# Four K pairs of each up strip by seven products instead of three, two remainders by an adding transfer

## The reference, cut to what matters

```python
# x: (1, 256, 2048) float32
h = h + 0.5 * rms_norm(swiglu(rms_norm(h, ffn1_pre), ffn1_up, ffn1_down), ffn1_post)
mix = hybrid_mixer(rms_norm(h, mix_pre), w_in, ...)      # pooling, window attention, retention; gated merge
h = h + rms_norm(mix, mix_post)
h = h + 0.5 * rms_norm(swiglu(rms_norm(h, ffn2_pre), ffn2_up, ffn2_down), ffn2_post)

def swiglu(x, w_up, w_down):                             # w_up: 2048 x 11264, w_down: 5632 x 2048
    g, u = jnp.split(x @ w_up, 2, axis=-1)
    return (jax.nn.silu(g) * u) @ w_down
```

## Time and profile before

| | us |
|---|---|
| median of 3 runs | 2365.75 (2365.57 to 2366.02) |
| the profiled execution | 2365.93 |
| its span, first to last instruction | 2364.2 |
| up loop of the first FFN, about | 60 to 477 |
| up loop of the second FFN, about | 1710 to 2127 |

### The profile page before, as it was taken

The page is one execution under the profiler, slowest core; times in us unless marked ns, Lnnn a source line. Parts: engine busy times, 40 slices in busy tenths (PEclk is TensorE's granted clock), DMA queues, the critical chain, the costliest instruction groups (busy, mean ns, idle before and its releaser), DMA issues. The chain is left out here.

```text
span 2364.2 us, 34093 instructions
## 1 busy us (share of the span) xinstructions
PE 2349.9 (99%) x10579; PEld 1938.5 (82%) x10579; DVE 1823.2 (77%) x2163; ACT 1265.4 (54%) x1519; POOL 207.0 (9%) x402
## 2 busy tenths in 40 slices
PE   9999999999999999999999999999999999999998
PEld 7888888888888888888888888888888888888887
DVE  5999999978876655656675767665799999997886
ACT  6555555555545554454555544544655555555553
POOL 1212112110000000000000000000021212111000
PEclk9999999999999999999999999999999999999999
DMA  7666676665676565565565566666666666666665
GB/s 236 218 212 206 216 222 215 220 214 192 207 242 210 159 182 172 160 188 158 178 200 192 195 195 203 194 240 198 204 210 225 213 214 207 218 213 214 205 204 196
DMA packets 267183, 481.64 MB, mean 204 GB/s; under 512 B 21217, under 2 KB 54673, under 8 KB 265457
## 3 DMA queue, kind: packets, MB, share of 16 engines
q1 hardware_dynamic: 252752, 453.04, 59.5%
q0 software_dynamic: 14192, 27.73, 3.5%
q10 hardware_dynamic: 176, 0.07, 0.0%
HBM read 462.93 MB, written 6.29 MB: 198 GB/s over the span
## 5 line engine op out<-in xcount | busy, mean ns | idle before, releaser
L1382 ACT ACTIVATE w_hi<-w_raw 128x1024 fp32r<-128x1024 f32 (+1 forms) x848 | 857.4, 1015 | 926.1 <-PE acc L843 627.9
L1778 DVE TENSOR_TENSOR w_lo<-w_raw,w_hi 128x1024 fp32r<-128x1024 f32 (+1 forms) x848 | 984.2, 1164 | 420.0 <-ACT w_hi L1382 415.5
L841 PE MATMUL acc<-w_hi,xT_hi 128*128 128x512 f32 x1376 | 540.9, 393 | 1.2 <-DVE w_lo L1778 1.0
L843 PE MATMUL acc<-w_hi,xT_lo 128*128 128x512 f32 x1376 | 535.9, 389 | 0.0
L842 PE MATMUL acc<-w_lo,xT_hi 128*128 128x512 f32 x1376 | 535.7, 389 | 0.0
L841 PEld LDWEIGHTS acc<-w_hi,xT_hi 128*128 128x128 f32 x1376 | 258.3, 188 | 56.7 <-issue 3.0
L843 PEld LDWEIGHTS acc<-w_hi,xT_lo 128*128 128x128 f32 x1376 | 258.3, 188 | 54.4
L842 PEld LDWEIGHTS acc<-w_lo,xT_hi 128*128 128x128 f32 x1376 | 258.4, 188 | 52.2
L753 POOL DMA_DIRECT2D act_raw<-blocks x352 | 174.9, 497 | 736.3 <-DVE blocks L2114 646.9
L841 PE MATMUL acc<-w_hi,act_hi 128*128 128x512 f32 x560 | 218.2, 390 | 0.1
L842 PE MATMUL acc<-w_lo,act_hi 128*128 128x512 f32 x560 | 217.9, 389 | 0.0
(11 more groups left out here) (321 smaller groups left out, 2866.0 us busy)
## 6 DMA issues: line engine op xcount, KB each, us to landing
w_raw<-in_ffn_up_dram SPq DMA_DIRECT2D x352, 512.0 KB, 4.2
w_raw<-in_ffn_down_dram SPq DMA_DIRECT2D x176, 512.0 KB, 4.2
w_raw<-in_w_gate_dram SPq DMA_DIRECT2D x96, 512.0 KB, 4.4
w_raw<-in_w_in_dram SPq DMA_DIRECT2D x72, 512.0 KB, 3.7
w_raw<-in_w_in_dram SPq DMA_DIRECT2D x128, 256.0 KB, 3.0
w_raw<-in_w_ret_out_dram SPq DMA_DIRECT2D x32, 512.0 KB, 4.1
w_raw<-in_w_out_dram SPq DMA_DIRECT2D x32, 512.0 KB, 4.5
act_raw<-blocks POOLq DMA_DIRECT2D x352, 32.0 KB, 3.8
```

Source lines behind the costliest of these rows:

```text
L841: pe.matmul(pair[m][:, :], xh, wh, start=(first and kk == 0), stop=False)
L843: mm = pe.matmul(pair[m][:, :], xl, wh, start=False, stop=(last and kk == KG - 1))
L1382: act.activation(w_hi[:, s, cols], w_raw[:, s, cols], ACT.Copy).then_inc(w_rounded, 1)
L1778: dve.tensor_tensor(w_lo[:, s, cols], w_raw[:, s, cols], w_hi[:, s, cols].bitcast(f32), ALU.subtract).then_inc(w_split, 1)
```

## The change

QUADS gets a fourth entry, and the strip a new order: gate groups 0 to 3 plain, upper group 4 plain, quads (5, 6) and (7, 8), upper group 9 plain, quads (10, 11) and (12, 13), upper groups 14 and 15 plain. The remainders of groups 9 and 14 are no longer made by DVE: their raw weights go by SP into buffers of their own (`far_raw`), ACT writes the rounded weights and also their negative (`far_lo` = -hi), and POOL issues a transfer from `far_raw` to `far_lo` that adds (raw - hi). These are issued behind `turn_hidden` of the strip. PE waits for them ahead of groups 9 and 14 (`far_added`). The two sets of t buffers alternate, and `s_hi` and `far_lo` lie where `h` is at other times.

```diff
-QUADS = ((5, 6, 5), (9, 10, 6), (12, 13, 7))
-PLAIN_GATE = ((0, 0), (1, 1), (2, 2), (3, 3), (4, 4))
-PLAIN_UP = ((7, 0), (8, 1), (11, 2), (14, 3), (15, 4))
+QUADS = ((5, 6, 4), (7, 8, 5), (10, 11, 6), (12, 13, 7))
+ADDED = {9: (6, 1), 14: (10, 7)}
+PLAIN_GATE = ((0, 0), (1, 1), (2, 2), (3, 3))
+PLAIN_UP = ((4, 0), (9, 1), (14, 2), (15, 3))
...
-        T_SLOT = (1, 0, 1)
+        T_SLOT = (0, 1, 0, 1)
...
+                        if n in ADDED_LOAD:
+                            j = ADDED_AT[ADDED_LOAD[n]]
+                            sp.wait_ge(w_used, group(f"up{f}", i, ADDED_LOAD[n]) - 2 * GD + 1 + SLOTS)
+                            sp.dma_start(far_raw[j][:, :].rearrange("p (kk n) -> p kk n", kk=KG),
+                                         cols(ADDED_LOAD[n])).then_inc(far_landed[j], 16)
+                        if n in ADDED:
+                            sp.wait_ge(w_split, group(f"up{f}", i, n) + 1)
+                            sp.sem_inc(w_landed[n % SLOTS], 16)
+                        else:
+                            load(f"up{f}", i, n, cols(n))
...
+            def add_raw(f, i, n):
+
+                j = ADDED_AT[n]
+                pool.wait_ge(far_negated[j], strip_no(f"up{f}", i) + 1)
+                pool.sem_inc(far_begun, 1)
+                pool.dma_start(far_lo[j][:, :].bitcast(f32), far_raw[j][:, :], accum_op=ALU.add).then_inc(far_added[j], 16)
...
-            with pool.Fori(0, NUP) as p:
-                turn_hidden(0, p)
+            with pool.Fori(0, NST) as i:
+                turn_hidden(0, i)
+                for n in ADDED:
+                    add_raw(0, i, n)
+            turn_hidden(0, NST)
...
                         if n in up_of:
                             s, k = n % SLOTS, KG * up_of[n]
+                            if k == 0:
+                                pe.wait_ge(acc_read[pair_of(sec, 1)], strip_in_pair(sec, i, 1) + 1)
                             pe.wait_ge(w_split, group(sec, i, n) + 1 + SLOTS)
+                            if added(sec, n):
+                                pe.wait_ge(w_rounded, group(sec, i, n) + 1)
+                                pe.wait_ge(far_added[ADDED_AT[n]], 16 * (strip_no(sec, i) + 1))
...
+                    if added(sec, ahead):
+                        j = ADDED_AT[ahead]
+                        act.wait_ge(far_landed[j], 16 * (strip_no(sec, i) + 1))
+                        act.wait_ge(w_used, group(sec, i, ahead) + 1)
+                        act.activation(w_hi[:, s, :], far_raw[j][:, :], ACT.Copy).then_inc(w_rounded, 1)
+                        return
...
                         round_group(sec, i, n)
+                        if n in ADDED_NEGATE:
+                            j = ADDED_AT[ADDED_NEGATE[n]]
+                            act.wait_ge(far_landed[j], 16 * (strip_no(sec, i) + 1))
+                            act.wait_ge(w_used, group(sec, i, ADDED_NEGATE[n]) - 2 * GD + 1 + SLOTS)
+                            act.activation(far_lo[j][:, :], far_raw[j][:, :], ACT.Copy, scale=-1.0).then_inc(far_negated[j], 1)
...
                 s, cols = n % SLOTS, w_cols(sec, i, n + SLOTS)
+                if added(sec, n + SLOTS):
+                    return
+                groups = 2 if added(sec, n + SLOTS + 1) else 1
                 dve.wait_ge(w_rounded, group(sec, i, n + SLOTS) + 1)
-                dve.tensor_tensor(w_lo[:, s, cols], w_raw[:, s, cols], w_hi[:, s, cols].bitcast(f32), ALU.subtract).then_inc(w_split, 1)
+                dve.tensor_tensor(w_lo[:, s, cols], w_raw[:, s, cols], w_hi[:, s, cols].bitcast(f32),
+                                  ALU.subtract).then_inc(w_split, groups)
```

More of the change, by code:

```diff
@@ L51 @@
 WARM_UP = 2
-QUADS = ((5, 6, 5), (9, 10, 6), (12, 13, 7))
-PLAIN_GATE = ((0, 0), (1, 1), (2, 2), (3, 3), (4, 4))
-PLAIN_UP = ((7, 0), (8, 1), (11, 2), (14, 3), (15, 4))
+QUADS = ((5, 6, 4), (7, 8, 5), (10, 11, 6), (12, 13, 7))
+ADDED = {9: (6, 1), 14: (10, 7)}
+ADDED_LOAD = {at: n for n, (at, neg) in ADDED.items()}
+ADDED_NEGATE = {at: n for n, (load, at) in ADDED.items()}
+ADDED_AT = {n: j for j, n in enumerate(ADDED)}
+PLAIN_GATE = ((0, 0), (1, 1), (2, 2), (3, 3))
+PLAIN_UP = ((4, 0), (9, 1), (14, 2), (15, 3))
 NQUAD = len(QUADS)
@@ L254, in hybrid_trunk @@
         s_lo = sb("s_lo", [P, 4, NQUAD, P], f32r, at=s_x)
-        s_hi = sb("s_hi", [P, 4, NQUAD, P], f32r, at=s_x + 16 * NQUAD * P)
-        assert s_x + 32 * NQUAD * P <= r_end
+        s_hi = sb("s_hi", [P, 4, NQUAD, P], f32r, at=x_at - 4 * MT * D)
+        assert s_x + 16 * NQUAD * P <= r_end
+        far_raw = [sb("far_raw0", [P, KG * STRIP], f32, at=s_x + 16 * NQUAD * P),
+                   sb("far_raw1", [P, KG * STRIP], f32, at=r_hi - 4 * KG * STRIP)]
+        far_at = x_at - 4 * MT * D + 16 * NQUAD * P
+        far_lo = [sb(f"far_lo{j}", [P, KG * STRIP], f32r, at=far_at + 4 * KG * STRIP * j) for j in range(len(ADDED))]
+        assert s_x + 16 * NQUAD * P + 4 * KG * STRIP <= r_end and far_at + 8 * KG * STRIP <= x_at
         h_scaled = sb("h_scaled", [P, S_TILES * P], f32, at=r_hi)
@@ L396, in hybrid_trunk @@
         hid_split = sem("hid_split")
+        far_landed = [sem(f"far_landed{j}") for j in range(len(ADDED))]
+        far_negated = [sem(f"far_negated{j}") for j in range(len(ADDED))]
+        far_added = [sem(f"far_added{j}") for j in range(len(ADDED))]
+        far_begun = sem("far_begun")
         h_parked = sem("h_parked")
@@ L547, in w_cols, with t_row, added, strip_no @@
             return slice(STRIP, KG * STRIP) if half else slice(0, KG * STRIP)
+        def t_row(j, y):
+            swapped = QUADS[j][0] % SLOTS == SLOTS - 1 and y < 2
+            return 1 - y if swapped else y
         def t_pair(a, j, pair):
             return a[:, T_SLOT[j], 2 * pair:2 * pair + 2, :]
+        def added(sec, n):
+            return sec in ("up0", "up1") and n in ADDED
+        def strip_no(sec, i):
+            return NST * ("up0", "up1").index(sec) + i
         T_AT = {ng - 3 + pair: (j, pair) for j, (ng, nu, k) in enumerate(QUADS) for pair in range(2)}
@@ L815, in _ @@
             rsqrt("pre2", rs_pre[:, 2, :])
-            with pool.Fori(0, NUP) as p:
-                turn_hidden(1, p)
+            with pool.Fori(0, NST) as i:
+                turn_hidden(1, i)
+                for n in ADDED:
+                    add_raw(1, i, n)
+            turn_hidden(1, NST)
             wait_strip_read(pool, "up1", NST - 1, 1)
@@ L938, in scaled_transposes @@
                 pe.wait_ge(h_scaled_ready, f + 1)
-                for b, tiles in ((2, range(0, 2)), (3, range(2, S_TILES))):
+                for b, tiles in ((2, range(0, 4)), (3, range(4, S_TILES))):
                     claim(f"s{f}", b)
@@ L962, in tt @@
                 def tt(y):
-                    return t_hi[:, T_SLOT[j], y, :], t_lo[:, T_SLOT[j], y, :]
+                    return t_hi[:, T_SLOT[j], t_row(j, y), :], t_lo[:, T_SLOT[j], t_row(j, y), :]
                 if first:
@@ L972, in seven_products @@
                 three(gate[0][:, :], *x(1), *w(ng, 1), False, last).then_inc(w_used, 1)
-                if first:
-                    pe.wait_ge(acc_read[pair_of(sec, 1)], strip_in_pair(sec, i, 1) + 1)
                 pe.wait_ge(w_split, group(sec, i, nu) + 1 + SLOTS)
                 pe.wait_ge(s_split, f + 1)
-                three(upper[0][:, :], *s(3), *w(nu, 1), first, False).then_inc(w_used, 1)
+                three(upper[0][:, :], *s(3), *w(nu, 1), False, False).then_inc(w_used, 1)
                 pe.wait_ge(t_split, 2 * quad(f, i, j) + 1)
@@ L1121, in swiglu @@
                                     mm = three(acc[pair_of(sec, 1)][m][:, :], xT_hi[:, k + kk, rows], xT_lo[:, k + kk, rows],
-                                               w_hi[:, s, cols], w_lo[:, s, cols], m == 1 and k + kk == 0,
+                                               *weights_of(sec, n, cols), k + kk == 0,
                                                n == 2 * GD - 1 and kk == KG - 1)
```

35 lines of the change are left out of this document (23 added, 12 removed).

## The result

The changed kernel takes 2477.48 us (median of 4 runs), the one before 2365.89: ratio 1.0466, 95% interval 1.0448 to 1.0484. It is 4.7% slower. Slower was forecast, with 2431 and a range to 2470; the time lies above both.

A forecast was written before the change was run, and what follows sets the result against it. The prediction took PE's matmuls to bound the kernel, with DVE's late pieces making PE wait. A strip of 40.80 + 1.50 + 2.42 = 44.72 us against 41.48, over 20 strips, adds 64.8 to 2365.93: 2431 us, range 2382 to 2470.

The forecast's parts named there:

- What bounds the kernel: Whole kernel: paced by PE's matmuls, PE busy 99% of the span; a matmul less is time less unless PE waits.
- PE's saving: Each up-stage strip: 180 matmuls for 183, saving 0.68 us a strip, 13.6 us in all, the whole possible gain.
- DVE tied to PE at S + 6.55: S is PE's strip start; DVE's run begins with group 4's remainder at S + 6.55 and cannot start earlier.
- the first deadline: First quad's sixth product, S + 17.00: second half of t_lo ends at S + 17.80, so PE waits 0.80 us.
- The second deadline: Third quad's second-half t_lo, wanted at S + 29.24, is 1.50 us late, including the earlier 0.80; strip at least 42.30 us.
- The load of group 11: Third quad's first sum: load lands 0.67 us late undisturbed, 2.42 with 1.75 for the adding transfer; strip 44.72 us.
- ACT's 27.5 us: ACT's work in a strip: some 27.5 of 44 us, from 23.3, hidden under its waits for PE.
- PE and the added remainder: Ahead of group 9: transfer issued at S + 16.0, wanted at S + 23.12; landing after 7.9 us costs nothing of its own.
- The bound of 11.0 us: Group 9's adding transfer: costs nothing of its own until its landing passes 11.0 us.
- the heavier adding transfer: Rival at group 11's load: transfer weighs 1,024 KB or more, strips 46.47 us, 2466 us; heavier or slow together 0.17.
- the upper end of 2470: Top of the kernel time's range, set just past the 1,024 KB case of 2466 us.
- The sign: Whole kernel: slower 0.91, same 0.04, faster 0.05.

The follow-up runs named there:

- The filled kernel: Changed kernel plus twelve zero-tile matmuls on PE ahead of its wait for the second half of t_lo of the third quad; 2468.8 us, ratio 1.0429.
- the kernel with the adding transfer of 9 first: Changed kernel, but POOL issues the adding transfer of group 9 before the turning's 16 small transfers, not behind them; 2426.9 us, ratio 1.0254.
- the two halves of t_lo first: Changed kernel, but DVE makes the second half of t_lo of quads one and three before the next quad's first sum; 2451.9 us, ratio 1.0361.

## Why the prediction was wrong

**What bounds the kernel; PE's saving.** Right. A strip of the changed kernel has 180 matmul starts for 183 before, and where nobody waits the matmuls keep their 0.23 us. (The x183 of the window above is no count of a strip: 181 start in it, and it counts also those that reach into it.) The 13.6 us of saving were never to be seen, because no strip ran without a wait.

**DVE tied to PE at S + 6.55, the first deadline.** Right to 0.01 us: 16.59 for 16.58, and PE waits there. The profile has 0.63 to 0.71 us of idle time in most strips, counted from the end of the matmul ahead; from start to start it is 1.02 to 1.09 us, so 0.8 to 0.87 more than 0.23, for 0.80.

**The second deadline without a disturbed load.** Right in place; 42.30 was counted and mostly 42.5 to 42.8 measured without adding transfers. Some of the difference is PE's restart behind a wait (0.34 us to the second matmul at 125.35, not 0.23), 0.22 us for the two of a strip, which the sum did not have.

**The load of group 11.** Right in place, and the sum nearly right by two errors that cancel: undisturbed it lands after 3.5 to 4.1, mostly 3.6 to 3.8, not 4.2, and the adding transfer costs it 2.6, not 1.75. It landed after 6.15 for 5.95 forecast, and the first sum began at S + 23.27 for 23.02. Strips of 45.19 for 44.72: 0.25 of the difference is this sum, 0.22 the two restarts. (ACT's 27.5 us does not follow from its terms, which give 27.0; the window from 107.5 to 152.7 has 26.12. Nothing hangs on it.)

**PE and the added remainder.** Right for 18 strips, where the transfer lands after 5.9 to 6.8 us. Wrong for two: the forecast had no pause of POOL in it, and there it lands after 9.1 us from a start that is 3 us late, 12.2 us behind the S + 16.0 that was counted. The bound of 11.0 us itself is not contradicted.

**What is said of all the rest: that PE's wait costs its own length.** This is the step that failed, and it stood nowhere in the sum: 20 x (44.72 - 41.48) takes every matmul behind a wait at 0.2267 us. The clock falls with the wait. In the changed kernel there are 20 waits of PE of 3.0 to 4.2 us in the strips, and with 15 of them the granted clock is 0.50 for a stretch, which begins between 1.1 us ahead of the wait's end and 1.5 behind it; with 21 waits between 0.5 and 1.7 us it never is. In the two up stages 120 matmuls start 0.43 us apart, which costs 23.9 us. The filled kernel shows that the wait is the cause. By this count the time without them would be about 2454: still above 2431, but inside the range.

The account, measured distance by distance: the 18 distances between `hid_sb` starts are 95.3 us longer than before, and the forecast has 18 x 3.24 = 58.3 for them. Of the 37 missing, 8.6 are the strip itself (45.20 for 44.72), 20.0 the lowered clock in the 14 ordinary strips (46.63 - 45.20), 5.2 the two seventh strips, 2.8 the two last. The two first strips and what lies around them give 15.9 us for 6.5. In the account by distances the clock's part in the seventh and first strips is not separated. In the range the heavier adding transfer had been allowed for, but not this: the upper end of 2470 was made of one mechanism's bounds only. The sign was safe with any of these.

## What to carry to other kernels

When two engines are both nearly full, count the second one's work not in sum but from its last tie to the first up to each deadline; the one deadline that fails sets the strip, and work taken off elsewhere does not help. A scheme that frees 0.68 us of one engine and adds 1.95 to the other turns 2.7 us of idle time a strip, which had absorbed late loads and pauses, into almost none, and then small disturbances are paid. And price a wait of TensorE not by its length alone: behind one of 3 us the next matmuls may come at half speed, so several short waits can be cheaper than one long one of the same sum, though each brings its own restart of 0.11 us. Filling a wait with idle matmuls pays only where the wait is always there.

## What the runs showed of the hardware that was not expected

The granted clock fell after some waits and not after others of the same length: of the waits of 3.04 to 3.10 us in the changed kernel, those that end at 187.67 and 279.62 are followed by 0.50 and those that end at 234.46 and 326.39 are not. In the kernel with the adding transfer of 9 first, 5 of 8 waits of about 1.8 to 2.7 us had a fall as well, and a sixth at one of 2.9. No wait up to 1.7 us of that kernel or the changed one has a fall. What decides was not tried here.

An adding transfer of 512 KB within SBUF landed after 4.7 us in the second place of a strip. In the first place, behind the turning, it took 5.9 us and more in the changed kernel, with the load of group 11 issued 0.9 us behind it, but 4.8 with the two halves of t_lo first, where that load comes 2.0 us behind it; 9.1 with the second adding transfer 4.2 us behind it. The load shows the same: it lands 2.6 us later than without the transfer when it is issued 0.9 us behind it, and after 4.2 to 4.8 us, mostly some 0.8 later than without, when it is issued 2.0 us behind it. So in these two kernels one microsecond more between the two took away most of the delay.

POOL pauses for 3.04 us once a stage, in the eighth turning of the loop, in the kernel after; the filled kernel has 3.04 and 3.05 there, and a delay of that size stands in the kernel before too. Smaller ones stand elsewhere, as 1.67 us in a turning of the kernel before (at 1846.05). The profile names nothing for them.
